# Rotary embedding without TensorE and attention scores as three split products, in a two-layer diffusion backbone on one core

## The chip, the cores and the metric

The kernel runs on 1 core of one Trainium2 chip. Times are device microseconds. The kernel before takes 1282.69 us, median of 3 runs (1281.11 to 1283.16).

## What is computed

Two layers work on 256 latent tokens and 256 context tokens of 1024 channels. Each layer normalises and modulates its input, projects it with one matrix, runs four branches (windowed attention with rotary embedding and a sink, a convolution module, a short gated convolution, a Fourier mix), gates and merges them, and ends with a gated MLP. In the last layer only the latent tokens go beyond the keys and values. What matters here:

```python
def apply_rope(x, cos, sin):
    b, s, h, _ = x.shape
    xs = x.astype(jnp.float32).reshape(b, s, h, 2, 2, ROPE_FREQS)
    rot = jnp.stack([-xs[..., 1, :], xs[..., 0, :]], axis=-2)
    return (xs * cos + rot * sin).reshape(b, s, h, HEAD_DIM).astype(x.dtype)

def attend_with_sink(q, k, v, sink, mask):
    s = jnp.einsum("bqhgd,bkhd->bhgqk", q, k, preferred_element_type=jnp.float32) * (HEAD_DIM ** -0.5)
    if mask is not None:
        s = jnp.where(mask, s, NEG_INF)
    sk = sink.astype(jnp.float32)[None, :, :, None, None]
    m = jnp.maximum(jnp.max(s, axis=-1, keepdims=True), sk)
    p = jnp.exp(s - m)
    denom = jnp.sum(p, axis=-1, keepdims=True) + jnp.exp(sk - m)
    return jnp.einsum("bhgqk,bkhd->bqhgd", (p / denom).astype(v.dtype), v)
```

There are 8 query heads and 2 key heads of 64 channels; only latent queries and keys are rotated.

## The kernel before

**Layout and products.** Activations lie with channels on the 128 partitions and tokens (256 latent, then 256 context) along the row. Every weight is split: ScalarE copies the raw chunk to `w_hi` in fp32r (L1022), VectorE subtracts to get `w_lo` (L1340), and TensorE makes hi x hi, hi x lo and lo x hi (L547 to L549), each in one pass. A "chunk" is 128 output channels, 8 input tiles, so 24 matmuls: 128x512 in layer 0 (both streams), 128x256 in layer 1 (latent only).

**Order.** Each layer walks phases of chunks: `in` (18), `fn` (8), `sc` (8), `at` (12), `cf` (8), `out`, `up0`, `dn0`, `up1`, `dn1`. On each engine the code is a plain sequence by chunk index. There are 4 slots for weights and 4 PSUM banks `psA`. In step n ScalarE and VectorE make the weights of chunk n + 3, and VectorE then evacuates chunk n. SyncE issues all loads in chunk order (L433); a load waits until the slot's former weights were split (`rest_done`), and everything behind it on SyncE's queue waits too. In layer 0 the loads alternate with those of the adaLN weights (L407), which VectorE multiplies (L1361) and folds (L1372).

**The `in` phase** makes q (chunks 0 to 3), the Fourier input (4, 5), the gated convolution's inputs (6 to 11), k (12), v (13) and the convolution module's (14 to 17). In layer 1, during steps 0 to 7, VectorE also normalises the context stream for chunks 12 and 13: `scaled` (L1481), then ScalarE's `h_hi` (L1089), then `shifted_rest` (L1488). **Rotary** is done behind the steps of `ROT_AT`: TensorE multiplies a 128x256 tile of q or k with the matrix `rot`, which moves and signs the partners 16 partitions away, in plain fp32 (L779, recorded as two instructions), into `psB[1]` or `psB[3]`; VectorE multiplies that by `sin` (L1594), the tile by `cos` (L1596) and adds (L1598). The Fourier channels product (L738) follows chunk 10 and waits for the fourth rotary add.

**Attention** runs in "places", one for each chunk of `fn` and `sc` and a few of `at`, beside the gate products. One batch is 128 queries of a pair of heads: head t on partitions 0 to 63, head t + 4 on 64 to 127. Layer 0 has 16 batches, one each place, in turn latent queries (512 keys) and context queries (256 keys); layer 1 has 8 batches of 512 keys, one every two places. In place k TensorE makes the gate product of the chunk (24 matmuls), the scores of batch k (L807, two fp32 matmuls of 64 rows, one for each half, 4 recorded instructions), the mask (L813), the values of batch k - 2 (L835), the transposes ("turn") of batch k - 1 (L823), and the chunk's 6 branch products. VectorE in the place: `w_lo`, a convolution tap (L1611), `peak` (L1624 to L1630), the remainder of an attention output (L1644), a tap, `weight_sum` (L1636, L1638), the gated product (L1681). ScalarE: `share` (L1179), `w_hi`, the gate's tanh (L1222), copies, the exponentials (L1168). GpSimd does the other 31 taps of the convolution, two instructions each (L505, L507).

## Time and profile before

| | before |
|---|---|
| time, median of 3 runs | 1282.69 us (1281.11 to 1283.16) |
| the profiled execution | 1284.79 us, span 1282.8 us |
| granted TensorE clock | 0.998 |
| TensorE, weight loads | busy 1255.4 us, 1087.4 us |
| VectorE, ScalarE, GpSimd | busy 882.7, 554.0, 304.7 us |

Start times are microseconds from the span's start. A matmul's duration includes the time that its data takes through the array, so neighbours overlap; what one costs is read from start to start. "x4" merges neighbouring instructions of a line. Brackets give the idle time in front of an instruction and who ended it. Groups by line give the count, busy us and mean ns of one, and then the idle time before them.

### The profile page before, as it was taken

How to read it: one execution, taken by the hardware profiler on the slowest of the kernel's cores; microseconds unless marked ns; L12 is line 12 of the kernel's file. 1: busy time of each engine (PE TensorE's matmuls, PEld its weight loads, DVE VectorE, ACT ScalarE, POOL GpSimd, SP SyncE). 2: the span in 40 equal slices, each digit the busy share in tenths (PEclk: the TensorE clock that was granted, in tenths of full speed). 3: DMA queues.
4: the chain of work that ended last, by engine and by line, in shares of the span. 5: the costliest groups of instructions: out<-in, count | busy, mean ns of one | idle time of the engine just before them, and what ended most of it. 6: DMA issues, size and time to landing. Idle time of an engine off the chain costs nothing.

```text
span 1282.8 us, 19935 instructions
## 1 busy us (share of the span) xinstructions
PE 1255.4 (98%) x7682; PEld 1087.4 (85%) x7682; DVE 882.7 (69%) x1192; ACT 554.0 (43%) x874; POOL 304.7 (24%) x254
## 2 busy tenths in 40 slices
PE   5999999999999999999999999999999999999998
PEld 3688777777788898888888888898889998999998
DVE  4598878753699677663779774486787567765664
ACT  4223355554333245332223332244576545653553
POOL 0004499310142101111001110002693130220222
PEclk9999999999999999999999999999999999999999
DMA  9365511222356435563545664334433554674561
GB/s 379 135 219 180 177 62 63 74 66 67 119 185 237 131 100 173 188 200 117 176 145 189 210 200 146 113 114 153 158 121 105 183 174 132 189 218 151 182 221 40
DMA packets 49762, 198.49 MB, mean 155 GB/s; under 512 B 5520, under 2 KB 5904, under 8 KB 48528
## 3 DMA queue, kind: packets, MB, share of 16 engines
q1 hardware_dynamic: 49680, 197.36, 46.6%
q8 instruction: 56, 0.92, 0.3%
q14 instruction: 26, 0.21, 0.1%
HBM read 196.29 MB, written 1.05 MB: 154 GB/s over the span
## 4 chain that ended last, share of the span: by engine, by line
PE 90%; DVE 6%; ACT 2%; issue 1%; DMA 1%; SPq 0%; DVEq 0%; ACTq 0%
PE psA L547 26%; PE psA L549 25%; PE psA L548 25%; PE psB L547 2%; PE psB L549 2%; PE psB L548 2%; DVE w_lo L1340 2%; PE psB L823 1%; PE psB L835 1%; DVE acc L1611 1%; PE psA L807 1%; PE psB L568 1%; DVE small L1624 1%; ACT w_hi L1022 1%; DMA X<-x 1%
## 5 line engine op out<-in xcount | busy, mean ns | idle before, releaser
L547 PE MATMUL psA<-h_hi,w_hi 128*128 128x256 f32 (+1 forms) x1528 | 520.3, 341 | 3.7 <-DVE h_lo L1488 2.6
L549 PE MATMUL psA<-h_hi,w_lo 128*128 128x256 f32 (+1 forms) x1528 | 513.5, 336 | 0.0
L548 PE MATMUL psA<-h_lo,w_hi 128*128 128x256 f32 (+1 forms) x1528 | 513.2, 336 | 0.0
L1340 DVE TENSOR_TENSOR w_lo<-raw,w_hi 128x1024 fp32r<-128x1024 f32 (+2 forms) x244 | 337.6, 1384 | 90.1 <-ACT w_hi L1022 90.1
L1022 ACT ACTIVATE w_hi<-raw 128x1024 fp32r<-128x1024 f32 (+2 forms) x244 | 276.9, 1138 | 280.5 <-PE psA L549 202.0
L547 PEld LDWEIGHTS psA<-h_hi,w_hi 128*128 128x128 f32 x1528 | 291.5, 191 | 37.7 <-issue 5.3
L549 PEld LDWEIGHTS psA<-h_hi,w_lo 128*128 128x128 f32 x1528 | 291.4, 191 | 29.8
L548 PEld LDWEIGHTS psA<-h_lo,w_hi 128*128 128x128 f32 x1528 | 291.6, 191 | 28.7 <-issue 0.2
L532 POOL TENSOR_TENSOR hid_lo<-sig,hid_hi 128x512 f32 (+3 forms) x44 | 67.7, 1539 | 471.0 <-ACT hid_hi L1300 471.0
L1361 DVE SCALAR_TENSOR_TENSOR ada_sum<-raw,csil,ada_sum 128x1024 f32<-128x1024 f32 x112 | 154.8, 1412 | 0.0
L547 PE MATMUL psA<-hid_hi,w_hi 128*128 128x256 f32 (+1 forms) x352 | 116.0, 330 | 0.0
L549 PE MATMUL psA<-hid_hi,w_lo 128*128 128x256 f32 (+1 forms) x352 | 116.0, 329 | 0.0
L548 PE MATMUL psA<-hid_lo,w_hi 128*128 128x256 f32 (+1 forms) x352 | 115.9, 329 | 0.0
L507 POOL TENSOR_TENSOR acc<-acc,sqb 128x512 f32<-128x512 f32 (+1 forms) x60 | 75.5, 1258 | 5.0
L1311 ACT ACTIVATE tmp<-psA,vec 128x512 f32<-128x512 f32 (+1 forms) x44 | 29.6, 672 | 108.0 <-PE psA L549 108.0
L1766 DVE SCALAR_TENSOR_TENSOR X<-psA,mod,X 128x256 f32<-128x256 f32 x52 | 23.8, 479 | 76.1 <-PE psA L549 76.1
L1796 DVE SCALAR_TENSOR_TENSOR tmp<-psA,vec,tmp 128x510 f32<-128x510 f32 (+1 forms) x44 | 27.1, 615 | 70.7 <-ACT tmp L1311 70.6
L547 PEld LDWEIGHTS psA<-hid_hi,w_hi 128*128 128x128 f32 x352 | 66.9, 190 | 6.1
L548 PEld LDWEIGHTS psA<-hid_lo,w_hi 128*128 128x128 f32 x352 | 66.9, 190 | 6.0
L549 PEld LDWEIGHTS psA<-hid_hi,w_lo 128*128 128x128 f32 x352 | 66.9, 190 | 6.0
L513 POOL TENSOR_TENSOR X<-X,tmp 128x512 f32<-128x512 f32 (+1 forms) x28 | 44.5, 1596 | 100.4 <-DVE tmp L1681 52.9
L513 POOL TENSOR_TENSOR X<-X,gtmp 128x512 f32<-128x512 f32 (+1 forms) x20 | 25.7, 1289 | 122.5 <-DVE gtmp L1681 77.7
(206 smaller groups left out, 1490.9 us busy)
## 6 DMA issues: line engine op xcount, KB each, us to landing
raw<-w_up SPq DMA_DIRECT2D x88, 512.0 KB, 4.3
raw<-w_ada SPq DMA_DIRECT2D x80, 512.0 KB, 3.5
raw<-w_dn SPq DMA_DIRECT2D x32, 704.0 KB, 4.4
raw<-w_in SPq DMA_DIRECT2D x36, 512.0 KB, 4.5
raw<-w_at SPq DMA_DIRECT2D x24, 512.0 KB, 3.4
raw<-w_fn SPq DMA_DIRECT2D x16, 640.0 KB, 4.0
raw<-w_sc SPq DMA_DIRECT2D x16, 640.0 KB, 3.9
raw<-w_cf SPq DMA_DIRECT2D x16, 640.0 KB, 4.0
```

The costliest lines, as they stand in the source:

```text
L507: pool.tensor_tensor(dst, dst, part, ALU.add).then_inc(tap_pool, 1)
L513: pool.tensor_tensor(dst, dst, src[:, 0:T], ALU.add).then_inc(m_sum, 1)
L532: pool.tensor_tensor(dst, sig[b][:, 0:T], src.bitcast(F32), ALU.subtract)\
L547: pe.matmul(out, w0, hi, start=first, stop=False)
L548: pe.matmul(out, w0, lo, start=False, stop=False)
L549: return pe.matmul(out, w1, hi, start=False, stop=last)
L1022: act.activation(w_hi[:, s, 0:tiles * P], raw[:, r, 0:tiles * P], ACT.Copy).then_inc(head_done, 1)
L1311: act.activation(tmp[b][:, 0:T], psA[st.slot][:, 0:T], ACT.Identity, bias=Vd("ffn_b", st.up(p0 + pair, 2)), scale=Vd("ffn_w", st.up(3 * (p ...
L1340: dve.tensor_tensor(w_lo[:, s, 0:tiles * P], raw[:, r, 0:tiles * P], w_hi[:, s, 0:tiles * P].bitcast(F32), ALU.subtract).then_inc(rest_don ...
L1361: op = dve.scalar_tensor_tensor(dst, w, c, dst, ALU.mult, ALU.add)
L1766: op = dve.scalar_tensor_tensor(dst, bank[:, cols], g, src, ALU.mult, ALU.add)
L1796: dve.scalar_tensor_tensor(t3[:, :, 1:SEQ], p3[:, :, 0:SEQ - 1], Vd("ffn_w", st.up(w, 6)), t3[:, :, 1:SEQ], ALU.mult, ALU.add).then_inc(cv, 1)
```

## The change

- The weight columns of q and k are permuted on the host, within each head, so that the two rotary partners lie in neighbouring partitions (even and odd); the sine table carries the sign, the tables are permuted alike. The matrix `rot` is gone.
- SyncE swaps the partners: `swap_pairs` waits for the evacuation of q chunk j (or k, chunk 12) and issues two transfers, 64 partitions of 1 KB each, into a scratch tile (`sig` halves, or `sqa`). They stand in front of the loads of the chunks in `SWAP_AT`. The `fn` loads of layer 1 are written out one by one instead of a loop, since one swap falls among them.
- VectorE's three rotary operations read the swapped tile instead of PSUM. In layer 1 the four of q move from behind steps 5 to 8 to behind steps 8 to 11 (behind the normalisation of the context stream); k's moves from 14 to 15 in both layers. TensorE has no rotation and none of its waits; the Fourier channels wait for the eighth evacuation.
- Scores: k is split once a layer into `k_hi` (ScalarE, 128x512) and `k_lo` (VectorE); q is split for each batch, 128x128, into two buffers in turn, two batches ahead. The scores are three fp32r products (hi hi, hi lo, lo hi) for each half instead of one fp32 product, halves in turn. ScalarE's copy for batch k + 2 stands behind the exponentials of batch k, VectorE's difference behind the gated product of that place.

```diff
 
-ROT_AT = {5: 0, 6: 1, 7: 2, 8: 3, 14: 4}
+ROPE_AT = [{5: 0, 6: 1, 7: 2, 8: 3, 15: 4}, {8: 0, 9: 1, 10: 2, 11: 3, 15: 4}]
+SWAP_AT = [{8: 0, 9: 1, 10: 2, 11: 3, 18: 4}, {8: 0, 9: 1, 10: 2, 11: 3, 20: 4}]
...
+        q_hi = place("q_hi", [2, P], F32R)
+        q_lo = place("q_lo", [2, P], F32R)
         ada_part = place("ada_part", [2, P * KD // 32])
         assert top[0] <= nc.sbuf_usable_end, (top[0], nc.sbuf_usable_end)
 
...
+        k_lo = at("k_lo", [NT], F32R, k_off)
+        k_hi = at("k_hi", [NT], F32R, sqa_off)
         x_in = at("x_in", [KD, NT], F32, q_off)
...
+        swap = [sig[j // 2][:, SEQ * (j % 2):SEQ * (j % 2 + 1)] for j in range(4)] + [sqa[:, 0:SEQ]]
         qsig = [q[:, b, :] for b in range(2)]
...
-            sp.dma_start(mat[:, MAT["rot"]:NMAT], io["mat"][:, MAT["rot"]:NMAT]).then_inc(mats_late, 16)
+            sp.dma_start(mat[:, MAT["chan"]:NMAT], io["mat"][:, MAT["chan"]:NMAT]).then_inc(mats_late, 16)
             sp.dma_start(acc[:, 0, 0:2 * P], io["band"]).then_inc(band_in, 16)
+            def swap_pairs(layer, j):
+
+                sp.wait_ge(evac, layer * PER_LAYER + (j if j < 4 else 12) + 1)
+                src = q[:, j, 0:SEQ] if j < 4 else k_all[:, 0:SEQ]
+                for h in range(2):
+                    sp.dma_start(swap[j][h:P:2, :], src[1 - h:P:2, :]).then_inc(swapped[j], 16)
+
             for layer in range(DEPTH):
                 for name, _, tiles in PHASES:
                     src = io[f"w_{name}{layer}"]
...
                     def load(st):
                         if st.n < FIRST_LEAD:
                             return
+                        if st.i is None and st.n - layer * PER_LAYER in SWAP_AT[layer]:
+                            swap_pairs(layer, SWAP_AT[layer][st.n - layer * PER_LAYER])
                         p = PLACE[("w", st.n)]
                         slot_free(p, 0 if st.i is None else SLOTS * st.i)
                         dst = raw[:, p % SLOTS, 0:tiles * P]
...
 
-                    walk(sp, layer, name, load, skip=LEN[name] if layer == 0 or name == "in" else 0)
+                    walk(sp, layer, name, load, skip=LEN[name] if layer == 0 or name in ("in", "fn") else 0)
                     if layer == 0 and name == "cf":
 
...
 
-                    pe.wait_ge(rope, 15 * layer + 12)
-                    pe.wait_ge(evac, n0 + 6)
+                    if layer == 0:
+                        pe.wait_ge(mats_late, 16)
+                    pe.wait_ge(evac, n0 + 8)
                     for tb in range(T // P):
...
-                    if idx in ROT_AT:
-
-                        j = ROT_AT[idx]
-                        if layer == 0 and j == 0:
-                            pe.wait_ge(mats_late, 16)
-                        pe.wait_ge(evac, n0 + (j if j < 4 else 12) + 1)
-                        if j >= 2:
-                            pe.wait_ge(rope, 15 * layer + 3 * (j - 2) + 1)
-                        if j == 4:
-                            pe.wait_ge(fn_rest, fc0 + 2 * streams(layer))
-                        src = q[:, j, 0:SEQ] if j < 4 else k_all[:, 0:SEQ]
-                        pe.matmul(psB[1 + 2 * (j % 2)][:, 0:SEQ], M("rot"), src, start=True, stop=True)\
-                            .then_inc(rot, 1)
                     if idx == 10:
                         fourier_channels()
                     if idx == 12:
...
-                        pe.wait_ge(rope, 15 * (layer + 1))
+                        pe.wait_ge(k_rest, layer + 1)
                         pe.wait_ge(v_done, layer + 1)
                         pe.wait_ge(evac, n0 + 16)
                         pe.wait_ge(band_done, 2)
                     else:
                         pe.wait_ge(expd, 3 * (b0 + k - 1) + 2)
-                    for half in range(2):
-                        rows = slice(64 * half, 64 * half + 64)
-                        mm = pe.matmul(score_bank(layer, half)[:, 0:nk * P], q[rows, t, q0:q0 + P],
-                                       k_all[rows, k0 * P:(k0 + nk) * P], start=True, stop=True)
-                        if s == 1:
-                            mm.then_inc(s_mm, 1)
+                    pe.wait_ge(q_rest, b0 + k + 1)
+                    b = (b0 + k) % 2
+                    for part, (qs, ks) in enumerate(((q_hi, k_hi), (q_hi, k_lo), (q_lo, k_hi))):
+                        for half in range(2):
+                            rows = slice(64 * half, 64 * half + 64)
+                            mm = pe.matmul(score_bank(layer, half)[:, 0:nk * P], qs[rows, b, :],
+                                           ks[rows, k0 * P:(k0 + nk) * P], start=(part == 0), stop=(part == 2))
+                            if s == 1 and part == 2:
+                                mm.then_inc(s_mm, 1)
                     if s == 0:
                         for half in range(2):
                             pe.matmul(score_bank(layer, half)[:, (1 - qi) * P:(2 - qi) * P], band[:, 2, :],
...
+
+                def query_head(k):
+
+                    if k >= len(un):
+                        return
+                    s, qi, t = un[k]
+                    q0 = SEQ * s + P * qi
+                    if b0 + k >= 2:
+                        act.wait_ge(q_rest, b0 + k - 1)
+                        act.wait_ge(s_mm, 2 * (b0 + k) - 2)
+                    act.activation(q_hi[:, (b0 + k) % 2, :], q[:, t, q0:q0 + P], ACT.Copy).then_inc(q_head, 1)
+
+                act.wait_ge(rope, 15 * (layer + 1))
+                act.activation(k_hi[:, :], k_all[:, :], ACT.Copy).then_inc(k_head, 1)
+                for k in range(2):
+                    query_head(k)
                 act.wait_ge(nsink_done, 1)
 
                 def weigh(k, half):
...
                             attend(place)
+                            if layer == 0 or place % 2:
+                                query_head(place // (1 + layer) + 2)
                         if name == "fn" and st.idx in (4, 5):
...
                         dve.tensor_copy(v[:, :, :].rearrange("p b n -> p (b n)"), psB[2][:, :]).then_inc(v_done, 1)
-                    if idx in ROT_AT:
-
-                        j = ROT_AT[idx]
+                    if idx in ROPE_AT[layer]:
+
+                        j = ROPE_AT[layer][idx]
                         dst = q[:, j, 0:SEQ] if j < 4 else k_all[:, 0:SEQ]
                         r = 15 * layer + 3 * j
-                        dve.wait_ge(rot, 5 * layer + j + 1)
-                        if j >= 2:
-                            dve.wait_ge(rope, r - 3)
-                        dve.tensor_tensor(tmp[j % 2][:, 0:SEQ], psB[1 + 2 * (j % 2)][:, 0:SEQ], M("sin", SEQ),
-                                          ALU.mult).then_inc(rope, 1)
+                        if layer == 0 and j == 0:
+                            dve.wait_ge(mats_late, 16)
+                        dve.wait_ge(swapped[j], 32 * (layer + 1))
+                        dve.tensor_tensor(swap[j], swap[j], M("sin", SEQ), ALU.mult).then_inc(rope, 1)
                         dve.tensor_tensor(dst, dst, M("cos", SEQ), ALU.mult).then_inc(rope, 1)
                         dve.wait_ge(rope, r + 2)
-                        dve.tensor_tensor(dst, dst, tmp[j % 2][:, 0:SEQ], ALU.add).then_inc(rope, 1)
+                        dve.tensor_tensor(dst, dst, swap[j], ALU.add).then_inc(rope, 1)
                     if layer == 0:
                         ada_behind(st)
+
+                un, b0 = batches(layer), B0[layer]
+
+                def query_rest(k):
+
+                    if k >= len(un):
+                        return
+                    s, qi, t = un[k]
+                    q0 = SEQ * s + P * qi
+                    dve.wait_ge(q_head, b0 + k + 1)
+                    dve.tensor_tensor(q_lo[:, (b0 + k) % 2, :], q[:, t, q0:q0 + P],
+                                      q_hi[:, (b0 + k) % 2, :].bitcast(F32), ALU.subtract).then_inc(q_rest, 1)
+
+                dve.wait_ge(k_head, layer + 1)
+                dve.tensor_tensor(k_lo[:, :], k_all[:, :], k_hi[:, :].bitcast(F32), ALU.subtract).then_inc(k_rest, 1)
+                for k in range(2):
+                    query_rest(k)
 
                 def conv_tap(j):
 
...
                                               y_hi[:, 2 + c, 0:T].bitcast(F32), ALU.subtract).then_inc(sc_rest, 1)
+                        if place is not None and (layer == 0 or place % 2):
+                            query_rest(place // (1 + layer) + 2)
                         if layer == 0:
...
         for half in range(2):
-            a[axis * 32 + half * 16:axis * 32 + half * 16 + 16] = pos[axis][None, :] * inv[:, None]
+            a[axis * 32 + half:axis * 32 + 32:2] = pos[axis][None, :] * inv[:, None]
     m[:, MAT["cos"]:MAT["cos"] + SEQ] = np.tile(np.cos(a), (2, 1))
-    m[:, MAT["sin"]:MAT["sin"] + SEQ] = np.tile(np.sin(a), (2, 1))
+    side = np.where(np.arange(P) % 2 == 0, -1.0, 1.0)[:, None].astype(np.float32)
+    m[:, MAT["sin"]:MAT["sin"] + SEQ] = np.tile(np.sin(a), (2, 1)) * side
     return m
 
...
         wq, wk, wv, wcf, wb, wc, wx, wf = (tiles(w[:, s:e]) for s, e in zip(at[:-1], at[1:]))
-        wq = tiles(w[:, heads])
+        wq = tiles(w[:, heads].reshape(D, N_HEADS, 2, 2, HEAD // 4).swapaxes(3, 4).reshape(D, -1))
+        wk = tiles(w[:, Q_W:Q_W + KV_W].reshape(D, KV_W // HEAD, 2, 2, HEAD // 4).swapaxes(3, 4).reshape(D, -1))
         gates = tiles(w[:, at[-1]:]).reshape(4, KD, KD, P, P)
```

## Rows read from the trace of the kernel before

**Rows 1.** page, part 1: engine, busy us (share of the span), instructions
```profile
PE 1255.4 (98%) x7682; PEld 1087.4 (85%) x7682; DVE 882.7 (69%) x1192; ACT 554.0 (43%) x874; POOL 304.7 (24%) x254
```

**Rows 2.** page, part 4: chain of work that ended last, by engine
```profile
PE 90%; DVE 6%; ACT 2%; issue 1%; DMA 1%; SPq 0%; DVEq 0%; ACTq 0%
```

**Rows 3.** timeline, TensorE: start us, us, engine, line, operation [idle before <-releaser]
```profile
865.16 0.67 PE L779 MATMUL psB<-q,mat 128*128 128x256 f32 x2 [1.02 <-DVE tmp L1594]
...
875.88 0.70 PE L738 MATMUL psB<-mat,X 128*128 128x256 f32 x2 [0.59 <-DVE q L1598]
```

**Rows 4.** timeline, VectorE, layer 1's input projection
```profile
858.81 1.22 DVE L1340 TENSOR_TENSOR w_lo<-raw,w_hi 128x1024 fp32r<-128x1024 f32 x1 [0.47 <-ACT w_hi L1022]
...
861.95 1.22 DVE L1340 TENSOR_TENSOR w_lo<-raw,w_hi 128x1024 fp32r<-128x1024 f32 x1 [0.41 <-ACT w_hi L1022]
...
864.60 0.41 DVE L1594 TENSOR_TENSOR tmp<-psB,mat 128x256 f32<-128x256 f32 x1
...
865.73 1.22 DVE L1340 TENSOR_TENSOR w_lo<-raw,w_hi 128x1024 fp32r<-128x1024 f32 x1
```

**Rows 5.** chain of work (start, us), layer 0's attention; third row: TensorE's timeline
```profile
201.83 0.71 ACT prob L1179
...
212.00 0.49 ACT prob L1179
...
221.33 0.94 PE L823 MATMUL psB<-mat,prob 128*128 128x128 f32 x5 [0.28 <-ACT prob L1179]
...
229.44 1.07 PE psA L807 x4
...
248.30 1.06 PE psA L807 x4
```

**Rows 6.** by line (busy us, mean ns): VectorE 155:221, 240:300; GpSimd 155:221
```profile
L1611 DVE SCALAR_TENSOR_TENSOR acc<-glu,vec,acc 128x512 f32<-128x512 f32 x13 | 18.3, 1405 | 0.0
...
L1611 DVE SCALAR_TENSOR_TENSOR acc<-glu,vec,acc 128x512 f32<-128x512 f32 x13 | 9.7, 743 | 0.0
...
L507 POOL TENSOR_TENSOR acc<-acc,sqb 128x512 f32<-128x512 f32 x26 | 40.5, 1558 | 2.2
```

**Rows 7.** timeline, TensorE, layer 0, around the first rotation
```profile
73.23 0.39 PE L548 MATMUL psA<-h_lo,w_hi 128*128 128x512 f32 x1
73.46 0.40 PE L549 MATMUL psA<-h_hi,w_lo 128*128 128x512 f32 x1
...
74.36 0.39 PE L548 MATMUL psA<-h_lo,w_hi 128*128 128x512 f32 x1
```

**Rows 8.** timeline, TensorE, layer 1's first rotation lies between the last two
```profile
857.14 0.28 PE L548 MATMUL psA<-h_lo,w_hi 128*128 128x256 f32 x1
857.26 0.28 PE L549 MATMUL psA<-h_hi,w_lo 128*128 128x256 f32 x1
...
857.93 0.28 PE L548 MATMUL psA<-h_lo,w_hi 128*128 128x256 f32 x1
```

**Rows 9.** DMA issues: tile, queue, count, KB each, median us to landing
```profile
out<-y_out SPq DMA_DIRECT2D x4, 256.0 KB, 2.5
```

**Rows 10.** timeline, TensorE, layer 0: first scores, band, second scores, turn
```profile
154.75 1.13 PE L807 MATMUL psA<-k,q 64*128 64x512 f32 x4
155.81 0.28 PE L813 MATMUL psA<-band 128*128 128x128 bf16 x2
...
163.35 0.70 PE L807 MATMUL psA<-k,q 64*128 64x256 f32 x4
163.98 1.09 PE L823 MATMUL psB<-mat,prob 128*128 128x128 f32 x8
```

**Rows 11.** timeline, VectorE: idle before first scores, a w_lo, layer 1's scores
```profile
156.07 1.29 DVE L1624 TENSOR_REDUCE small<-psA 128x1 f32<-128x512 f32 x2 [2.54 <-PE psA L813]
...
203.73 1.50 DVE L1340 TENSOR_TENSOR w_lo<-raw,w_hi 128x1280 fp32r<-128x1280 f32 x1 [1.96 <-ACT w_hi L1022]
...
909.95 1.29 DVE L1624 TENSOR_REDUCE small<-psA 128x1 f32<-128x512 f32 x2 [3.58 <-PE psA L813]
```

More of the change, by code:

```diff
@@ L203, in program @@
         q = place("q", [4, NT])
+        k_off = top[0]
         k_all = place("k", [NT])
@@ L1612, in conv_tap @@
                     op.then_inc(tap, 1)
-                un, b0 = batches(layer), B0[layer]
                 def peak(k):
```

18 lines of the change are left out of this document (7 added, 11 removed).

## The prediction

> **What bounds the kernel now.** I read the page first. TensorE is busy for 98% of the span [rows 1] and the chain of work that ended last lies on it for 90%; VectorE has 6% of that chain [rows 2]. So a microsecond saved on TensorE is a microsecond of the kernel, except in the stretches where VectorE's part lies. The reader should then look for these stretches, because the change adds work to VectorE and ScalarE and takes it from TensorE. In the chain in order of time there are two. One is layer 1's input projection from about 860 to 876 us, where VectorE's step (weight remainder, context stream's normalisation, evacuation, rotary) is what TensorE waits for [rows 3, 4]. The other is layer 0's attention from 155 to 221 us, where a loop "ScalarE share, ScalarE w_hi, VectorE w_lo, conv tap, peak, exp, weight_sum, share" takes 10.2 us for one place (201.83 to 212.00), while TensorE, where it isn't held up, needs 18.86 us for two places, 9.4 each (229.44 to 248.30) [rows 5]. In the latter stretch both are nearly level: TensorE is held there for some tenths of a microsecond now and then (0.28 us at 221.33), not more. After 221 us the loop has caught up, since GpSimd's taps end soon and VectorE's own tap falls from 1.4 to 0.74 us [rows 6].
>
> **Part 1: the rotation leaves TensorE.** In layer 0 a 128x512 matmul of the projection follows the next by 0.23 us, and with a rotation between them two such steps take 0.90 us (73.46 to 74.36) [rows 7]: the rotation costs 0.90 - 2 x 0.226 = 0.45 us. No wait lies there, so five rotations give 2.25 us, all on the path, since TensorE is continuously fed from 60 to 155 us. What is late next would be VectorE; TensorE's chunk shrinks to 5.45 us (24 matmuls x 0.227), but w_lo is made three chunks ahead, 16 us, and VectorE's work is the same as before. So I cost this at nothing, and a cover gone would cost no more than the 2.25 us.
>
> In layer 1 the matmuls follow each other by 0.12 us, and the rotation costs 0.67 - 0.24 = 0.43 us [rows 8]. Here there are waits too: TensorE sits idle 1.02 us before the third rotation until the first rotary product has freed its buffer, and again before the Fourier channels until the last rotary add (0.59 us by the row, 0.75 us against the usual pitch) [rows 3]. The change removes both reasons: no rotation waits, and the Fourier channels wait for the eighth evacuation alone. What is late next is the weight remainder w_lo. Before the first rotary work of layer 1 VectorE's steps start 3.14 us apart (858.81, 861.95); with rotary work the next comes 3.78 us later (865.73), the three products taking 1.13 us (864.60 to 865.73) [rows 4]. With rotary at steps 8 to 11 the pitch stays 3.14 for the rest of the normalisation. Chunk 10 needs the w_lo of step 7: 861.95 + 2 x 3.14 + 1.22 = 869.45 us. TensorE alone, at the end of chunk 5 at 857.38 (857.26 + 0.12) [rows 8], would have it begin at 857.38 + 4 x 2.88 = 868.9 us (24 x 0.12 = 2.88 us a chunk). So it ends at 869.45 + 2.88 = 872.3 us, and the Fourier channels start some 872.4 us instead of 875.88: 3.5 us gained, of which 1.7 us are four rotations and 1.8 us waits. Behind that, steps 8 to 11 cost VectorE 1.14 + 0.34 + 1.13 = 2.6 us each, less than TensorE's 2.88, and the wide chunks 12 and 13 (5.4 us each) let it catch up. The fifth rotation gives 0.4 us. Together **part 1 gives 2.25 + 3.5 + 0.4 = 6.2 us**; the bounds are 4.4 us (only the ten rotations) and 6.8 us (TensorE never held).
>
> **Part 2: SyncE's swaps.** Ten swaps of two transfers, each 64 partitions of 1 KB, 1.3 MB of the 198 in all. Each swap makes SyncE wait for an evacuation, and behind this are queued all weight loads. In layer 1 load 7+j is issued when w_lo of step j ends, and the evacuation of chunk j is about 0.8 us behind it; the next load can't go before 3.1 us later, and two issues take 0.33 us each, so nothing is late. In layer 0 the awaited evacuation is long past, or, for k, one step old. No such transfer is in the trace; the nearest is an output piece of 256 KB, which lands in 2.5 us with nothing in front of it [rows 9]; I take up to twice that, because the swap stands behind a weight load. The shortest margin is the first one of layer 0: issued near 68 us, wanted at 78.3 us. So I cost this at nothing; a swap would have to take four times the 2.5 us to be late at all, and each microsecond beyond would first eat VectorE's lead. The Trainium skill, "DMA: Bandwidth & Descriptors", section "Anatomy of one DMA", gives about 2.0 us fixed plus the bytes over 436 GB/s; that is an estimate of 2.2 us for one such transfer, and leaves the sum as it is.
>
> **Part 3: three split products for one fp32 product in the scores.** One batch's two halves (64 rows each) of 512 keys take 1.06 us (154.75 to 155.81), of 256 keys 0.63 us (163.35 to 163.98) [rows 10]. The difference, 0.43 us for 256 columns, is what one rotation costs, which is one fp32 product over 256 columns [rows 8]. So an fp32 product is four passes of 0.107 us for 256 columns, the two halves run side by side, and a fixed 0.20 us stands around them (1.06 - 8 x 0.107). The new form has per half three products of one pass. No row shows a single-pass product on 64 rows; the nearest are these fp32 halves (side by side) on one side and the full-height single-pass products (0.227 us for 512 columns, 0.12 for 256, one after another) on the other. If halves run side by side: 3 x 0.227 + 0.20 = 0.88 us, saving 0.18; and 3 x 0.12 + 0.20 = 0.56, saving 0.07. If they run one after another: 1.56 and 0.92 us, costing 0.50 and 0.29. I take the first, as it is the same pair of row halves and the same banks. Layer 0 has 8 batches of each kind, 8 x 0.18 + 8 x 0.07 = 2.0 us; layer 1 has 8 wide ones, 1.4 us. Up to 221 us the loop of [rows 5] sets the end, so the 1.0 us of the first half of layer 0 turn into waits before turn. **Part 3 gives 1.0 + 1.3 = 2.3 us.**
>
> **Part 4: splitting q and k.** Each batch adds a 128x128 copy on ScalarE and a 128x128 difference on VectorE; like forms (y_hi, y_lo of the attention output) take 0.26 and 0.28 us. Each layer adds a 128x512 pair of 0.6 and 0.69 us. Where they lie: VectorE's difference comes after the gated product and before w_lo, where VectorE waits 1.96 us for ScalarE [rows 11]; ScalarE's copy comes after the exp and before share, where ScalarE waits for weight_sum too. Both are hidden in the loop. At the start of attention VectorE waits for the first scores for 2.54 us in layer 0 and 3.58 us in layer 1 [rows 11]; added are 0.69 + 2 x 0.28 = 1.25 us. In layer 1 they stand in front of the scores now. VectorE is idle from 906.4 to 909.95 us, and the scores take the last 1.3 us of that, from 908.6. ScalarE's copy of k stands behind the load of the Exp table and I estimate its end at 906.6, so VectorE is through at 906.6 + 1.25 = 907.9. This holds by 0.7 us only. GpSimd runs its taps at that time, and a VectorE tap beside them takes 1.4 us instead of 0.74 [rows 6]; the new differences, and the rotary product that read PSUM and now reads the swapped copy, take two operands from SBUF as taps do. I allow 0.3 us for both layers; the bounds are 0 and 5 us.
>
> The Trainium skill speaks against the change here: "SBUF — State Buffer", section "SBUF: two separate sides", says that a VectorE instruction with two SBUF inputs and a GpSimd instruction that reads SBUF lock each other out for their whole length. The trace agrees as far as the taps go. By it, a small difference can wait for a whole GpSimd add, and that is the second rival below.
>
> **Sum.** 6.2 + 2.3 - 0.3 = 8.2 us. Made against the profiled execution, 1284.79 us with a span of 1282.8 us, it gives 1276.6. That execution lies 2.1 us over the median of the runs, 1282.69 us, from which I predict **1274.5 us**.
>
> **The rivals.**
> Rival A, slower: the two 64-row halves don't run side by side as single-pass products. For it: no row shows it. Against it: the fp32 halves do. Price: 8 x 0.50 + 8 x 0.29 in layer 0 and 8 x 0.50 in layer 1, 10.3 us, of which the waits that are there now (about 1.5 us) take up some, 8.8 us. With part 1, 1282.7 - 6.2 + 8.8 = **1285.3 us**. It decides from the point where the extra per batch, times 24, exceeds part 1, that is 0.26 us for a batch.
> Rival B: VectorE's loop grows. Each added difference waits for a GpSimd add of 1.56 us [rows 6]. In the loop's idle of 1.96 us even that fits (1.84 us), so the price is at the starts: three instructions with up to 1.56 us each are 4.7 + 1.25 = 5.9 us against 2.5 us of idle in layer 0, 3.4 us; in layer 1, where GpSimd's instructions are half as long, 1 us; and some tenths in each of seven places, 1 us. That is 5.4 us, so 1282.7 - 8.5 + 5.4 = **1279.6 us**. Against it: in layer 0 the split stands just behind GpSimd's start, so at most some of the three are hit.
> Rival C: the change doesn't do what it says to the waits: in layer 1 the held time comes back after the Fourier channels because VectorE's steps 8 to 11 start late. Then only the ten rotations and the scores pay, 4.4 + 2.3 - 0.3 = 6.4 us, **1276.3 us**.
>
> **How the numbers follow.** The forecast has 0.62, rival C 0.13, B 0.12, A 0.11; 0.02 is left for a swap that lands late. What a measurement of this kernel can tell from no change is about 0.2%, 2.6 us. Forecast and C are faster by more than that (0.75), B mostly (0.06 of 0.12 counted, the rest as within), A lies at +0.2%, half and half. So faster 0.81, within 0.2% 0.11, slower 0.08. The range reaches down by what part 1's upper bound (0.6), part 3 without the loop (1.1) and some more of side-by-side work would give, to 1271 us, and up over B with the whole 5 us of part 4 on top of rival C, to 1282 us; A is left out.
>
> **What would show each step.** The rotations' rows gone and chunk after chunk of layer 1's projection 2.9 to 3.1 us apart; the Fourier channels of layer 1 about 5.7 us earlier (3.5 and what layer 0 gave). The pair of score halves starting within some 10 ns, and a batch of 512 keys at 0.88 us: at 1.5 us rival A holds. The turn at place 7 of layer 0 as long behind the first scores as now, 66.6 us; more shows rival B. The first scores of layer 1 without idle in front. I would be wrong if single-pass products on half the rows are not side by side, or if VectorE or SyncE turn out to be what layer 0's projection waits for.

## The result, and the profile after

The changed kernel takes 1272.54 us (median of 5 runs, 1271.83 to 1275.71); the kernel before, beside it, 1281.79 us (5 runs, 1281.11 to 1283.16). The ratio is 0.9935, with a 95% interval of 0.9923 to 0.9947. The forecast was 1274.5 us and the range 1271 to 1282: direction and size were right. Of the 2.0 us between the forecast and the measured time, 0.9 us come from the kernel before, whose median is 1281.79 us here and was 1282.69 us when the forecast was made; 1.05 us are gain that the forecast left out (9.25 us gained, 8.2 forecast). The profiled execution took 1274.56 us with a span of 1272.8 us; beside the 1282.8 us of the profiled one of before that is 10.0 us.

Page of the changed kernel, the parts that answer to [rows 1, 2]:

```profile
PE 1244.9 (98%) x7710; PEld 1086.0 (85%) x7710; DVE 892.3 (70%) x1218; ACT 559.0 (44%) x900; POOL 307.0 (24%) x254
...
PE 91%; DVE 6%; ACT 2%; issue 1%; DMA 1%; SPq 0%; DVEq 0%; ACTq 0%
```

TensorE is busy for 10.5 us less and the span is 10.0 us shorter; VectorE is busy for 9.6 us more and has the same 6% of the chain. That fits the sum's idea, that a microsecond off TensorE is a microsecond of the kernel; but a part of both differences is chance in TensorE's clock, as the section on the start shows.

Where the time went shows when the starts of the same operations are subtracted, stage by stage. All numbers are us between two starts of TensorE in a kernel's own trace; layer 0's stages stand first, then layer 1's. "Merge" is the first product with the merged branches (mg_hi), "down" the first of layer 1's MLP with hid_hi.

| stage | before | after | gain |
|---|---|---|---|
| first psA product at | 24.47 | 23.49 | 0.98 |
| to layer 0's first Fourier product (four rotations in it) | 78.26 | 74.08 | 4.18 |
| to its first scores (the fifth rotation) | 52.02 | 51.57 | 0.45 |
| to its 16th scores | 140.77 | 141.07 | -0.30 |
| to its merge | 129.68 | 129.62 | 0.06 |
| to layer 1's first Fourier product | 450.68 | 447.31 | 3.37 |
| to its first scores | 32.74 | 32.22 | 0.52 |
| to its last scores | 71.02 | 69.78 | 1.24 |
| to its merge | 75.87 | 75.69 | 0.18 |
| to the MLP's down products | 92.86 | 93.55 | -0.69 |
| to the end | 134.33 | 134.32 | 0.01 |

TensorE's timeline of the changed kernel where [rows 3, 10] stood: layer 0's first scores (512 keys) and second (256 keys), then the Fourier channels of layer 1.

```profile
149.13 0.50 PE L817 MATMUL psA<-k_hi,q_hi 64*128 64x512 f32 x2
149.47 0.40 PE L817 MATMUL psA<-k_lo,q_hi 64*128 64x512 f32 x2
149.71 0.39 PE L817 MATMUL psA<-k_hi,q_lo 64*128 64x512 f32 x2
150.03 0.29 PE L823 MATMUL psA<-band 128*128 128x128 bf16 x2
...
157.56 0.39 PE L817 MATMUL psA<-k_hi,q_hi 64*128 64x256 f32 x2
...
158.11 0.66 PE L833 MATMUL psB<-mat,prob 128*128 128x128 f32 x4
...
867.01 0.28 PE L568 MATMUL psA<-h_hi,w_lo 128*128 128x256 f32 x1
867.13 1.24 PE L758 MATMUL psB<-mat,X 128*128 128x256 f32 x5
```

A batch of 512 keys takes 150.03 - 149.13 = 0.90 us to its band, one of 256 keys 158.11 - 157.56 = 0.55: the 0.88 and 0.56 of the forecast. "x2" on one row are the two halves, whose starts lie 2 to 4 ns apart. The Fourier channels of layer 1 follow the last product without the idle of [rows 3].

The swaps, which no row of before could show, as DMA issues (tile, queue, count, KB each, median us to landing):

```profile
sig<-q SPq DMA_DIRECT2D x16, 64.0 KB, 3.2
sqa<-k SPq DMA_DIRECT2D x4, 64.0 KB, 3.2
```

And what was not forecast, in layer 0's attention: TensorE, which before had two waits of 0.63 us together there (0.28 us at 221.33 in [rows 5], and the first row here), has three longer ones, 2.24 us together (the other rows).

```profile
201.97 1.27 PE L823 MATMUL psB<-mat,prob 128*128 128x128 f32 x8 [0.35 <-ACT prob L1179]
```

```profile
193.77 0.39 PE L568 MATMUL psA<-h_hi,w_lo 128*128 128x512 f32 x1
195.09 0.39 PE L817 MATMUL psA<-k_hi,q_hi 64*128 64x256 f32 x2 [0.93 <-ACT prob L1194]
...
197.03 1.27 PE L833 MATMUL psB<-mat,prob 128*128 128x128 f32 x8 [0.74 <-ACT prob L1205]
...
216.61 0.66 PE L833 MATMUL psB<-mat,prob 128*128 128x128 f32 x4 [0.57 <-ACT prob L1205]
```

Some of the expectations below count these waits as 0.93 us before and 2.93 us in four after; the brackets of the two traces give 0.63 and 2.24 us.

### The profile page after: what moved, and what is told of

Read it like the earlier page. It is cut to its first block, busy times and chain, and to the rows that moved or that the text cites. A ratio compares the mean times of both kernels' runs of the same rounds, so it can differ in the third digit from the quotient of the medians.

```text
span 1272.8 us, 20064 instructions
## 1 busy us (share of the span) xinstructions
PE 1244.9 (98%) x7710; PEld 1086.0 (85%) x7710; DVE 892.3 (70%) x1218; ACT 559.0 (44%) x900; POOL 307.0 (24%) x254
## 3 DMA queue, kind: packets, MB, share of 16 engines
HBM read 196.22 MB, written 1.05 MB: 155 GB/s over the span
## 4 chain that ended last, share of the span: by engine, by line
PE 91%; DVE 6%; ACT 2%; issue 1%; DMA 1%; SPq 0%; DVEq 0%; ACTq 0%
PE psA L566 26%; PE psA L567 26%; PE psA L568 26%; PE psB L566 2%; PE psB L568 2%; PE psB L567 2%; DVE acc L1655 1%; PE psB L845 1%; PE psB L833 1%; DVE w_lo L1368 1%; PE psA L817 1%; DVE small L1666 1%; PE psB L587 1%; DVE small L1669 1%; ACT w_hi L1032 1%
```

## Experiments

There are eleven experiments; two of them are repeats, of the changed kernel and of the kernel before. The kernel before, run beside them, took 1282.41 us (16 runs; beside the first four: the change once more, its two halves, and the steps left where they were), 1282.01 (9 runs; beside the order of the halves, the late taps in the changed kernel and the two without GpSimd's taps) and 1281.80 (29 runs; beside the last three).

### The whole change once more, and its two halves alone

The same kernel again, as the measure for all that follows:

> The changed kernel once more, beside the kernel before on the same chip, and the base for the runs of this group. In the first pair of profiles the changed kernel was 10.0 us shorter; of these 3.3 us came from the first 35 us (TensorE's clock was granted sooner) and 0.7 us were lost at a norm, so my theory puts 7.4 us on the change: 1274.5 us beside 1281.8. If the start is part of the change and no luck, it stays at 9 us or more below, 1272.5.

1272.79 us (6 runs, 1271.32 to 1276.21), ratio 0.9924 [0.991, 0.9938]: 9.6 us below the kernel before. The theory of 7.4 us is too low for the medians. The reason given for the other reading, that the early grant belongs to the change, is wrong as well, as the section on the start shows.

Only the swaps and the moved steps, with the scores in fp32 and no splits:

```diff
-                    pe.wait_ge(q_rest, b0 + k + 1)
-                    b = (b0 + k) % 2
-                    for part, (qs, ks) in enumerate(((q_hi, k_hi), (q_hi, k_lo), (q_lo, k_hi))):
-                        for half in range(2):
...
+                    for half in range(2):
+                        rows = slice(64 * half, 64 * half + 64)
+                        mm = pe.matmul(score_bank(layer, half)[:, 0:nk * P], q[rows, t, q0:q0 + P],
+                                       k_all[rows, k0 * P:(k0 + nk) * P], start=True, stop=True)
...
```

> The rotation by SyncE's swaps and the moved steps, with the scores as one fp32 product as before and no split of q and k. My theory: this carries 6.2 us of the gain (2.25 in layer 0, 3.5 at the Fourier channels of layer 1, 0.4 for k), so it lies 6.2 us below the kernel before and 1.2 us above the changed kernel. Rival: the split scores carry half, then it lies 4.4 us below before.

1275.78 us (6 runs, 1275.08 to 1278.05), ratio 0.995 [0.9938, 0.9962]: 6.6 us gained, where part 1 said 6.2; the interval allows 4.9 to 8.0. In its trace the stages that part 1 is about gain what they do in the whole change, and layer 0's attention, where no wait is left, takes 1.25 us less than before (139.52 for 140.77 us). Part 1 has no term for that, and no run here shows what took those waits away.

Only the split scores, with the rotation on TensorE as before:

```diff
-                    for half in range(2):
-                        rows = slice(64 * half, 64 * half + 64)
-                        mm = pe.matmul(score_bank(layer, half)[:, 0:nk * P], q[rows, t, q0:q0 + P],
...
+                    for part, (qs, ks) in enumerate(((q_hi, k_hi), (q_hi, k_lo), (q_lo, k_hi))):
+                        for half in range(2):
...
```

> The kernel before with the split scores alone, rotations and waits on TensorE kept. My theory: layer 0's attention is set by the loop of VectorE and ScalarE, so its 1.8 us saved on TensorE give nothing or lose 0.2 to 0.5; layer 1 gives 1.4 us; together 1.0 to 1.2 us below the kernel before, within 0.2%. Rival (parts add up to the median's 9 us): 3 us below.

1279.23 us (10 runs, 1277.85 to 1283.74), ratio 0.9977 [0.9967, 0.9986]: 3.2 us gained (the interval allows 1.8 to 4.2), not 1.0 to 1.2, so the rival of 3 us was right and the term was sized too low. The halves add up: 6.6 + 3.2 = 9.8 us against 9.6 for the whole.

### The steps of layer 1 left where they were

```diff
-ROPE_AT = [{5: 0, 6: 1, 7: 2, 8: 3, 15: 4}, {8: 0, 9: 1, 10: 2, 11: 3, 15: 4}]
+ROPE_AT = [{5: 0, 6: 1, 7: 2, 8: 3, 15: 4}, {5: 0, 6: 1, 7: 2, 8: 3, 15: 4}]
```

> The changed kernel with layer 1's four rotary steps of q left behind steps 5 to 8, in the midst of the context stream's normalisation, as before. My theory: VectorE's steps become 3.8 us there, chunk 10's w_lo is ready 1.2 us later than with the move, so it is 1.2 us slower than the changed kernel. Rival: the waits were TensorE's own rotation waits and go with it whatever the place, then no difference.

1274.45 us (6 runs, 1273.42 to 1277.22), 1.7 us over the whole change (expected 1.2); in its trace the stage to layer 1's first Fourier product takes 448.51 us instead of 447.31, which is the expected 1.2 to the tenth. So of the 3.37 us of that stage 2.2 come from the rotations being gone from TensorE and 1.2 from VectorE's rotary steps standing behind the context stream's normalisation.

### The order of the halves

```diff
-                    for part, (qs, ks) in enumerate(((q_hi, k_hi), (q_hi, k_lo), (q_lo, k_hi))):
-                        for half in range(2):
+                    for half in range(2):
+                        for part, (qs, ks) in enumerate(((q_hi, k_hi), (q_hi, k_lo), (q_lo, k_hi))):
```

> The changed kernel with the six score products of a block issued as three of the first half and then three of the second, instead of the halves in turn. Theory, that two products on the two halves of the partitions run side by side only when they are neighbours in the queue: only the third of the first half and the first of the second still overlap, so a block has five steps instead of three: 0.89 us grows by 2 x 0.227 to 1.34 for 512 keys, 0.55 by 2 x 0.12 to 0.79 for 256 keys; 16 x 0.45 + 8 x 0.24 = 9.1 us, less up to 2.9 us that layer 0's waits absorb: 1279 to 1282. If no halves overlap at all in this order it is six steps: 1283 to 1286. Rival, that the order makes no difference (the engine is not freed by a half's product at all, or it looks ahead): the blocks stay at 0.89 and 0.55 us and the time at 1272.8.

1272.49 us (5 runs, 1272.12 to 1276.02), ratio 0.9932 [0.9919, 0.9946]: no difference, and the rival was right, the theory wrong. TensorE's timeline of this kernel, first scores:

```profile
149.26 0.51 PE L817 MATMUL psA<-k_hi,q_hi 64*128 64x512 f32 x2
149.60 0.40 PE L817 MATMUL psA<-k_lo,q_hi 64*128 64x512 f32 x2
149.83 0.39 PE L817 MATMUL psA<-k_hi,q_lo 64*128 64x512 f32 x2
150.16 0.29 PE L823 MATMUL psA<-band 128*128 128x128 bf16 x2
```

The program has the products k_hi, k_lo, k_hi of the first half and then the same of the second, and yet the two k_hi,q_hi start together (one row, 10 ns apart), ahead of the first half's second product, 0.34 us later. A block takes the same 0.90 us. The halves don't need to be neighbours in the program: by these starts, products on the other half of the rows overtake those of the first half. Rival A of the prediction is out in either order.

### Who makes TensorE wait in layer 0's attention

Here part 3 and part 4 meet, and the split-only run says that one of them is mis-sized. (A tap is one of the convolution's 31 multiply-and-add steps that VectorE does, two at each place.) Three kernels take the suspects away. First, fewer VectorE taps at the early places:

```diff
+TAPS_AT = [[([], [p]) for p in range(8)] + [([8 + 2 * p], [9 + 2 * p]) for p in range(2)]
+           + [([12 + 3 * p], [13 + 3 * p, 14 + 3 * p]) for p in range(5)] + [([27, 28], [29, 30])],
...
-                            if 2 * place < CONF_K:
-                                conv_tap(2 * place)
+                            for j in TAPS_AT[layer][place][0]:
+                                conv_tap(j)
...
```

> The changed kernel with layer 0's 31 VectorE taps spread otherwise: one each at the attention's places 0 to 7 instead of two, two at places 8 and 9, three at 10 to 14, four at 15. In the changed kernel the stretch from layer 0's first scores to its 16th takes 141.07 us, of which 2.93 us are four TensorE waits between 193.8 and 224.8 us for prob (ScalarE); with fp32 scores and the swaps the same stretch has no such wait and takes 139.52 us. Theory, that VectorE's own loop (two taps of 1.07 us, a split, the share chain) is late at places 4 to 7 and sets these waits: one tap less there shortens each turn of the loop by about 1.07 us, the waits go, the stretch takes 138.1 to 138.5 us and the median falls by 2 to 2.9 us, to about 1270.3 (beside 1272.8). Rival, that the waits belong to ScalarE's and GpSimd's work or to the swaps: the waits stay and the time is within 0.5 us of 1272.8. A third outcome: the three taps of the places from 10 on make new waits there, and it is slower by 1 us or more.

1271.52 us (5 runs, 1271.19 to 1272.97), ratio 0.9922 [0.9908, 0.9935]. Second and third, 30 of GpSimd's 31 taps left out in each layer, with the split scores and with fp32 scores. The output of these two kernels lacks that part of the convolution:

```diff
-                for j in range(CONF_K):
...
-                    pool.tensor_scalar(part, src, w, 0.0, ALU.mult, ALU.add).then_inc(tap_pool, 1)
-                    pool.wait_ge(tap_pool, c0 + 2 * j + 1)
-                    pool.tensor_tensor(dst, dst, part, ALU.add).then_inc(tap_pool, 1)
...
+                pool.tensor_scalar(dst, glu[:, 1, 0:S, 0:SEQ], V("conf_w", TAPS * layer + CONF_K),
+                                   V("conf_b", 2 * layer + 1), ALU.mult, ALU.add).then_inc(tap_pool, POOL_STEPS)
```

> The changed kernel with 30 of the 31 convolution taps of GpSimd left out in each layer (their part of the convolution is missing from the output). Theory, that VectorE's operations beside a busy GpSimd are lengthened and this sets the four TensorE waits of 2.93 us in layer 0's attention: they go, the stretch from layer 0's first scores to the 16th falls from 141.07 to 138.1 us, layer 1's stays within 0.3 us of 69.78, and the median is 1269.5 to 1270.5. Rival, that VectorE's loop is late by its own work alone: the stretch stays above 140.5 us and the time within 0.5 us of 1272.8.

> The kernel with the swaps and the moved steps but fp32 scores without splits, and with 30 of GpSimd's 31 taps left out in each layer (their part of the convolution is missing). It gives the worth of the split scores where no wait takes part of it back. Theory: TensorE alone saves 1.4 us in layer 0 (139.52 less 138.14 us) and 1.25 us in layer 1, so this is 2.7 us slower than the kernel with split scores and the same taps left out, and within 0.5 us of the 1275.8 that it takes with the taps, since it has no waits to lose: 1275.3 to 1276. Rival: it is faster than 1275.8 by 1 us or more, which says that GpSimd's taps cost the fp32 scores as much as the split ones, and the layer 0 wait has another cause.

1271.13 us (4 runs, 1270.84 to 1271.75) and 1275.06 us (4 runs, 1274.20 to 1277.64). The waits go as the theories said, but the sizes were missed in all three: the stretch falls further than forecast (137.74, not 138.1 or more), layer 1's scores take 0.56 us less without GpSimd's taps (at most 0.3 expected), the medians fall less (1.0 to 1.4 us below the changed kernel's 1272.49, where 2 us or more were expected), and the two kernels without GpSimd's taps lie 3.9 us apart (2.7 expected). The windows from layer 0's first scores to the 16th, in the changed kernel, the one with late taps and the one with swaps alone (stretch, length, then busy us and instructions of PE, PEld, DVE, ACT, POOL, PEclk):

```profile
149.14:290.21 141.07, 138.77 (x810) 107.99 (x810) 107.77 (x182) 79.61 (x192) 80.74 (x66) 1.00 0.20 65
```

```profile
149.44:287.18 137.74, 137.74 (x811) 108.07 (x810) 96.94 (x180) 81.05 (x192) 79.36 (x66) 1.00 0.20 67
```

```profile
149.27:288.79 139.52, 139.52 (x779) 105.76 (x778) 100.80 (x167) 77.53 (x178) 80.16 (x65) 1.00 0.19 63
```

With late taps TensorE is busy for all of the 137.74 us, and so it is in the kernel without GpSimd's taps (137.74 us as well): either remedy takes every wait away. So the waits need both, VectorE's two taps a place and GpSimd working beside them; both alone are not enough, since the swap-only kernel has them and no wait. With fp32 scores it is busy for 139.52 us. So the split scores are worth 139.52 - 137.74 = 1.78 us in layer 0 where VectorE keeps up, and the changed kernel's profiled execution gives 141.07 - 137.74 = 3.33 us back. The median moves less than this: late taps take 1.0 us off the kernel that ran beside them with taps as in the change (1272.49), not 2 to 2.9, and the intervals of the two overlap. A part of the reason is in the next section: in the trace of that neighbour (1272.49) the stretch takes 139.22 us, only 1.48 more than with late taps. Who makes VectorE late, its small instructions tell: the tap, weight_sum and the split by line between the first scores and 216 us in the changed kernel, then the tap, the split and weight_sum in the kernel without GpSimd's taps (149.4 to 214 us):

```profile
L1655 DVE SCALAR_TENSOR_TENSOR acc<-glu,vec,acc 128x512 f32<-128x512 f32 x13 | 18.2, 1403 | 0.0
...
L1678 DVE TENSOR_TENSOR small<-small 128x2 f32<-128x2 f32 x7 | 6.5, 925 | 0.9 <-ACT small L1199 0.9
L1638 DVE TENSOR_TENSOR q_lo<-q,q_hi 128x128 fp32r<-128x128 f32 x6 | 2.8, 469 | 0.0
```

```profile
L1645 DVE SCALAR_TENSOR_TENSOR acc<-glu,vec,acc 128x512 f32<-128x512 f32 x14 | 10.4, 745 | 0.0
...
L1628 DVE TENSOR_TENSOR q_lo<-q,q_hi 128x128 fp32r<-128x128 f32 x7 | 2.0, 285 | 0.0
...
L1668 DVE TENSOR_TENSOR small<-small 128x2 f32<-128x2 f32 x7 | 1.1, 161 | 7.2 <-ACT small L1189 7.2
```

An instruction over two elements a partition (weight_sum, line 1678) takes 925 ns on average beside GpSimd's taps (the seven take 0.15 to 1.24 us each) and 161 without them; the split 469 and 285; the tap 1403 and 745. In the changed kernel weight_sum stands ahead of share in the loop, and share is what TensorE waits for. The Trainium skill, "SBUF — State Buffer", section "SBUF: two separate sides", says that a VectorE instruction with two SBUF inputs and a GpSimd instruction reading SBUF lock each other out for their whole length; this pair of kernels agrees, down to the instruction whose own work is 161 ns.

The pair also prices part 3 without any wait: 1275.06 - 1271.13 = 3.9 us by the medians; by the traces 1.78 us in layer 0, 70.43 - 69.22 = 1.21 in layer 1's scores and 0.18 + 0.07 around them, 3.2 us. With GpSimd's taps and late VectorE taps the traces say the same: 1.78 in layer 0 and 1.24 in layer 1's scores. The prediction's two terms before anything was taken off were 2.0 + 1.4 = 3.4 us.

The same taps in the kernel before:

> The kernel before with layer 0's VectorE taps spread as in the run that took them from the early places: one at places 0 to 7, two at 8 and 9, three at 10 to 14, four at 15. Before has two TensorE waits of 0.93 us in all in layer 0's attention, and 140.77 us from the first scores to the 16th, where the kernel with swaps and fp32 scores has none and takes 139.52. Theory, that these waits belong to VectorE's loop: they go and the stretch is 139.5 us, 1 to 1.3 us less than before, so 1281 beside 1282.2. Against the same taps in the changed kernel (1271.5) this gives the change without its waits in layer 0: 9.5 to 10. Rival: the waits are ScalarE's and stay, the time is within 0.4 us of before.

1281.38 us (12 runs, 1277.61 to 1284.08), ratio 0.9999 [0.9987, 1.0012]. In its trace the waits are gone and the stretch takes 139.52 us, 1.25 less than before, as expected; in the median only 0.4 us of it shows, inside the measurement's error. Between the two kernels with late taps the change is worth 1281.4 - 1271.5 = 9.9 us (9.5 to 10 expected). By the traces of kernels without a wait in layer 0's attention it is 6.2 us of part 1 and 1.78 + 1.24 + 0.18 + 0.07 of the scores, 9.5 us.

### What a wait costs beyond itself

The stretch of 141.07 us is not a constant of the program. The three traces with the very same layer 0 code (the change, the change once more, layer 1's steps left where they were) have 141.07, 141.33 and 139.52 us, the one with the halves in order 139.22; the waits add up to 2.24, 1.66, 0.58 and 0.56 us. In the second of them the waits do more. TensorE's timeline there, then windows of that kernel, same columns as above:

```profile
196.35 0.39 PE L817 MATMUL psA<-k_hi,q_hi 64*128 64x256 f32 x2 [0.93 <-ACT prob L1194]
...
198.30 1.73 PE L833 MATMUL psB<-mat,prob 128*128 128x128 f32 x8 [0.73 <-ACT prob L1205]
```

```profile
195.00:198.00 3.00, 1.63 (x16) 0.83 (x15) 2.67 (x6) 2.59 (x8) 2.82 (x3) 1.00 0.01 3
198.00:201.00 3.00, 2.70 (x11) 2.32 (x12) 1.25 (x3) 3.00 (x6) 2.73 (x4) 0.66 0.02 5
201.00:204.00 3.00, 3.00 (x12) 2.32 (x12) 2.97 (x5) 0.64 (x2) 2.82 (x3) 0.77 0.41 137
```

After waits of 0.93 and 0.73 us (196.35 and 198.30 us) the granted clock falls to its half level (1.2 GHz) for 3 x 0.34 x 2 + 3 x 0.23 x 2 = 3.4 us and TensorE does half the work in them, which I estimate at 1.7 us lost. In the changed kernel's first trace the same two waits (0.93 and 0.74 us) left the full level as it was. The split-only kernel has such a stretch too, from 202.6 to 206.0 us (granted clock 0.50), behind waits of 0.93 and 0.74 us. Waits of 0.37 and 0.74 us, in the kernel that makes the swaps twice, left the full level too, and the five kernels without waits in layer 0's attention have no such stretch. Whether this is why the changed kernel's 11 runs reach from 1271.3 to 1276.2 us and the five with late taps only from 1271.2 to 1273.0 is not shown, and the record speaks for a second cause: the kernel before with late taps has no wait there in its trace, and its 12 runs still reach from 1277.6 to 1284.1 us. The start (below) differs by up to 4 us between traces of like kernels.

### The swaps twice

```diff
     for h in range(2):
         sp.dma_start(swap[j][h:P:2, :], src[1 - h:P:2, :]).then_inc(swapped[j], 16)
+    sp.wait_ge(swapped[j], 64 * layer + 32)
+    for h in range(2):
+        sp.dma_start(swap[j][h:P:2, :], src[1 - h:P:2, :]).then_inc(swapped[j], 16)
...
```

> The changed kernel with each of the five swaps of a layer made twice: SyncE issues the pair of transfers, waits until it has landed (3.2 us for one pair in the trace of the changed kernel), and issues it again, so that a channel's partners arrive 3.2 us later and SyncE's weight loads behind it are issued 3.2 us later, ten times in all. Theory, that the swap lies wholly beside other work: the time stays within 0.5 us of 1272.8. Rival, that the turn of a chunk is late on VectorE, so that each delay of layer 1's Fourier channels passes through: 3.2 us for the last channel's turn, to about 1276. Rival, that SyncE's queue is the narrow place: 10 x 3.2 us less what the loads have in hand, over 1280.

1278.98 us (10 runs, 1277.53 to 1283.00): 6.2 us over the changed kernel. Neither the theory (within 0.5 us) nor the first rival (about 1276) holds; the second, SyncE's queue as the narrow place, forecast over 1280 and comes nearest, but only a part of 10 x 3.2 us shows. TensorE's timeline of this kernel names the two places:

```profile
151.91 0.50 PE L820 MATMUL psA<-k_hi,q_hi 64*128 64x512 f32 x2 [2.19 <-DVE q_lo L1641]
...
869.12 0.39 PE L569 MATMUL psA<-h_hi,w_hi 128*128 128x256 f32 x1 [1.33 <-DVE w_lo L1371]
```

A swap that lands 3.2 us later makes layer 0's first scores wait for 2.19 us (k's turn, then both splits, stand before them) and chunk 10 of layer 1 for 1.33 us, since the weight behind the swap in SyncE's queue is late. So as made, the swaps are hidden, but with about 1 us in hand at k of layer 0 and about 2 at layer 1's Fourier chunks, not with the "four times 2.5 us" that part 2 claimed. The stages that grew add up to 2.25 + 0.88 + 1.32 + 0.62 = 5.1 us, of which some is half-level clock (153.4 to 156.8 us) behind the first of these waits.

### The start

In the profiled pair the stage before layer 0's Fourier product gains 4.18 us, of which four rotations explain 1.8. The rest is TensorE's clock: the same product takes 0.63 us at half level (1.2 GHz) and 0.40 at full (2.4 GHz). Before, then after, then the kernel before once more:

```profile
34.48 0.63 PE L549 MATMUL psA<-h_hi,w_lo 128*128 128x512 f32 x1
...
36.77 0.40 PE L548 MATMUL psA<-h_lo,w_hi 128*128 128x512 f32 x1
```

```profile
29.65 0.40 PE L567 MATMUL psA<-h_lo,w_hi 128*128 128x512 f32 x1
```

```profile
29.50 0.39 PE L549 MATMUL psA<-h_hi,w_lo 128*128 128x512 f32 x1
```

> The kernel before, unchanged, for another look at its start. In the traces of the two kernels without swaps TensorE's products run at half level (1.2 GHz, 628 ns for a product of 512 columns) until 35 to 36.4 us, in the eight kernels with swaps until 29.7 to 32 us, though TensorE's work until then is the same. If the later grant belongs to these kernels, it comes at 35 to 36.5 us here too and the first Fourier product is 78 us behind the first product; if it is chance, this one may show 29 to 32 us and 75 us, and then 3 of the 10 us between the two profiled runs are not of the change. Time 1280 to 1284.

1282.1 us (8 runs, 1280.19 to 1284.26). The full level comes at 29.5 us here, not at 35, and the stage takes 75.96 us; 75.96 - 74.08 = 1.88 us, four rotations at 0.47. In the kernel before with late taps it is at full level from the first product on (23.28 us), 74.27 us in all. So the earlier grant is not of the change, and 4.18 - 1.88 = 2.3 us of this stage's gain are chance. So is the 0.98 us of the stage ahead of it, whose first product comes at 23.02 us in this trace of the kernel before. That is 3.3 of the profiled pair's 10.0 us. The other way round, 0.7 us are lost by chance in layer 1's MLP norm, where the half level lasts for one or two such stretches in either kernel (92.86 or 93.56 us for before). So the profiled pair has 10.0 - 3.3 + 0.7 = 7.4 us of the change itself, with layer 0's waits in it.

## Why the prediction was right

The forecast was right in its mechanism for parts 1 and 2 and in the unit prices of part 3. That the sum came so near is partly luck. It took off 1.3 us for VectorE's loop and the splits; against the 9.5 us of the traces without waits, the profiled execution lost 2.1 us, and the medians (9.25 to 9.9 us gained) show next to no loss.

**Part 1** was sized right in each term: 0.47 and 0.45 us for a rotation of layer 0 (0.45 forecast), 3.37 us for layer 1's Fourier channels (3.5), 0.52 for the fifth rotation (0.4). 1.88 + 0.45 + 3.37 + 0.52 = 6.2 us. The swap-only kernel gains 6.6 by the medians; its trace adds 1.25 us in layer 0's attention, which part 1 doesn't have. The argument that carried it was to ask what is late next: w_lo of step 7, not TensorE, set the new start. Rival C, whose time of 1276.3 needed that the waits come back, is out: no idle stands in front of layer 1's Fourier channels or behind them.

**Part 2** was right in its sum and wrong in its margin. The landing took 3.2 us, within the 2.5 to 5 taken from the rows (the estimate of 2.2 us beside the sum was 1.0 us too low), and no wait of TensorE in that trace names a swap. But the claim that a swap "would have to take four times the 2.5 us to be late" looked only at the first swap of layer 0; the narrow one is k's, whose turn now has two splits and the scores right behind it.

**Part 3** had its unit prices right (0.90 and 0.55 us for a batch, 0.88 and 0.56 forecast), and rival A is out. The sum writes layer 1's share once as 1.4 and once as 1.3 us; measured are 1.24 in its scores and 0.18 behind them. Its 2.3 us rest on "the 1.0 us of the first half of layer 0 turn into waits"; the profiled execution lost more than that (-0.30 us for the stretch of layer 0 where 0.7 was forecast), while the median of the split-only kernel gains 3.2 us, close to the full 3.4 with nothing taken off. Both fit if in most executions the loop of [rows 5] does not hold TensorE up as much as the first profiled one shows; the traces at 139.2 to 139.5 us, 1.2 to 1.6 us less than before, are of this kind. That most unprofiled runs are of this kind is argued from the medians and not shown by a trace.

**Part 4** named the right mechanism and the wrong place. The split's own cost in the loop is small (469 ns where 280 were taken). Beside it the two-element weight_sum grew to 925 ns from 820 in the kernel before; that this is because the loop now meets GpSimd's instructions at other moments was not tried by itself. The turn at place 7 came 67.5 us behind the first scores, 66.6 were to be seen: by the prediction's own mark this is rival B, but only in some executions (65.9 us in the trace with the same layer 0 code and one wait), at a smaller price than its 5.4 us and not in the starts: before layer 1's first scores TensorE has no idle at all, as forecast, and VectorE still waits 1.88 us for them where [rows 11] had 3.58.

So the errors had opposite signs: in the profiled execution the loop took more than was allowed (7.4 us in all, for 8.2 forecast), and by the medians the scores paid more than the 2.3 us of part 3 (9.25 to 9.9 us in all). The forecast lies between the two.

## What to carry to other kernels

When an operation leaves the bound engine, price it by the pitch between its neighbours, and then look for the next late thing in the same stretch: it, and not the removed work alone, gives the size of the gain. Beside a GpSimd chain on SBUF the time that a VectorE instruction with two SBUF inputs loses didn't follow its length here (0.76 us for 2 elements a partition, 0.18 for 128, 0.66 for 512, on average), so a tiny one that a critical engine waits for is worth a look. Short waits on TensorE were followed by a stretch at half clock in two of three traces with the same pair of waits, so even waits of 1 us in a stage that is otherwise fed are worth removing: moving eight taps to later places gave the lowest median of the complete kernels here, 1271.5 us, though its lead of 1.0 us over the changed kernel is within the measurement's error.

## What was not expected of the hardware

Single-pass fp32r products on 64 rows ran side by side with those on the other 64 in both orders of the program: 10 ns between the first products of both halves although two others stood between them in the program. The Trainium skill, "TensorE: Matmul & The Clock Gate", section "The mechanism", says of products that they keep strict program order; the kernel with one half after the other doesn't agree, since its fourth product starts 0.34 us before its second. The granted clock fell to its half level for 3.4 us after two waits of under 1 us each, in one execution of the changed kernel and in the split-only kernel; another execution of the changed kernel kept the full level behind the same two waits.
